# Ordering the gates in memory by group of four expert tiles

## What is computed

```python
    eidx = jnp.take_along_axis(cidx, pos, axis=-1)
    gates = jax.nn.softmax(top_s, axis=-1)
...
        u = jnp.take(u_tab, ib, axis=0)
        act = jax.nn.gelu(jnp.einsum('btd,bted->bte', hb, u), approximate=False)
        vv = jnp.take(v_tab, ib, axis=0)
        return jnp.einsum('bte,bted->btd', gb * act, vv)
```

## Time and profile before

| | |
|---|---|
| median of 3 runs | 2196.34 us (2192.71 to 2203.06) |
| profiled execution, its time / its span | 2198.44 us / 2196.6 us |
| TensorE busy in the span | 1880.5 us (86%) |
| VectorE busy | 1477.7 us (67%) |
| ScalarE busy | 729.6 us (33%) |
| moved by DMA | 411.22 MB in 160,491 packets |
| scatter stage's 12 writes | 994.5 to 1157.5 us (issue of first and last) |
| expert stage's gate loads | 1181.9 to 2111.4 us (issue of first and last) |

### The profile page before, as it was taken

The page is one execution under the profiler, slowest core; times in us unless marked ns, Lnnn a source line. Parts: engine busy times, 40 slices in busy tenths (PEclk is TensorE's granted clock), DMA queues, the critical chain, the costliest instruction groups (busy, mean ns, idle before and its releaser), DMA issues. The chain is left out here.

```text
span 2196.6 us, 33505 instructions
## 1 busy us (share of the span) xinstructions
PE 1880.5 (86%) x11429; PEld 1645.8 (75%) x11429; DVE 1477.7 (67%) x2682; ACT 729.6 (33%) x1060; POOL 709.8 (32%) x435
## 2 busy tenths in 40 slices
PE   2997678879986999968885998998998989989897
PEld 1765467768875999958874777787887878878797
DVE  5999544542313999999992667765766767768664
ACT  3235322233315444423432323332323323233233
POOL 1443111214442455521113222233443444435310
PEclk8999877779998999978997999999999998999999
DMA  7751000012222343324556888888888888788861
GB/s 298 261 180 48 1 2 0 0 38 94 97 77 77 132 136 131 123 76 169 191 205 245 310 294 297 295 284 307 279 265 296 275 305 279 263 311 283 296 212 57
DMA packets 160491, 411.22 MB, mean 187 GB/s; under 512 B 13496, under 2 KB 76088, under 8 KB 158784
## 3 DMA queue, kind: packets, MB, share of 16 engines
q1 hardware_dynamic: 115520, 264.13, 34.1%
q0 software_dynamic: 36864, 134.23, 18.6%
q10 hardware_dynamic: 8064, 12.32, 1.5%
HBM read 373.15 MB, written 37.49 MB: 187 GB/s over the span
## 5 line engine op out<-in xcount | busy, mean ns | idle before, releaser
L1645 PE MATMUL bank<-v_hi,coef_hi 128*128 128x512 f32 x768 | 305.0, 397 | 44.1 <-DVE coef_lo L1737 44.1
L1645 PE MATMUL bank<-v_hi,coef_lo 128*128 128x512 f32 x768 | 305.0, 397 | 0.0
L1645 PE MATMUL bank<-v_lo,coef_hi 128*128 128x512 f32 x768 | 304.9, 397 | 0.0
L1635 PE MATMUL bank<-h_hi,u_hi 128*128 128x384 f32 x608 | 220.1, 362 | 67.1 <-ACT gelu L1697 65.8
L1624 POOL DMA_INDIRECT own_rows<-in_u_rows_dram,own_row x128 | 154.8, 1209 | 349.6 <-DVE own_rows L1744 200.6
L1624 POOL DMA_INDIRECT own_rows<-in_peer_v_dram,own_row x128 | 189.8, 1483 | 230.4 <-DVE y_own L1801 217.4
L1635 PE MATMUL bank<-h_lo,u_hi 128*128 128x384 f32 x608 | 216.7, 356 | 0.0
L1635 PE MATMUL bank<-h_hi,u_lo 128*128 128x384 f32 x608 | 216.1, 355 | 0.0
L1737 DVE TENSOR_TENSOR v_lo<-v_tile,v_hi 128x1024 fp32r<-128x1024 f32 x128 | 156.2, 1220 | 76.5 <-ACT v_hi L1680 76.3
L1737 DVE TENSOR_TENSOR u_lo<-u_tile,u_hi 128x1024 fp32r<-128x1024 f32 x76 | 92.8, 1221 | 170.5 <-ACT u_hi L1674 170.5
L1645 PEld LDWEIGHTS bank<-v_hi,coef_hi 128*128 128x128 f32 x768 | 147.1, 192 | 78.0 <-issue 49.1
(11 more groups left out here) (326 smaller groups left out, 4106.2 us busy)
## 6 DMA issues: line engine op xcount, KB each, us to landing
v_tile<-in_peer_v_dram SPq DMA_DIRECT2D x128, 512.0 KB, 9.4
u_tile<-in_peer_u_dram SPq DMA_DIRECT2D x76, 512.0 KB
ada<-in_w_ada_dram SPq DMA_DIRECT2D x48, 512.0 KB, 4.9
gate_scratch<-gate_block SPq DMA_DIRECT2D x12, 2048.0 KB, 7.3
gate_tiles<-gate_scratch SPq DMA_DIRECT2D x32, 768.0 KB
piece<-in_peer_u_dram SPq DMA_DIRECT2D x36, 512.0 KB, 3.3
merge_w<-in_w_merge_dram SPq DMA_DIRECT2D x32, 512.0 KB, 3.3
wring<-in_w_proj_dram SPq DMA_DIRECT2D x28, 512.0 KB, 5.4
```

The lines of the kernel that those rows point to most:

```text
L1635: last = nc.tensor.matmul(bank[b][:, 0:TD], w[:, b, k, :], x[:, k, 0:TD], start=(k == 0 and n == 0), stop=(k == KT - 1 and n == 2))
L1645: last = nc.tensor.matmul(y_bank(t, half)[:], w[:, j, t * P:(t + 1) * P], x[:, j, c], start=(first and n == 0), stop=(final and n == 2))
```

## The change

`gate_scratch` keeps its size and contents, but not its order. Its axes were expert (partition), block of 32 tokens, tile, token. They are now expert, group of four tiles, block, tile in the group, token. A group's gates for one expert are so one contiguous piece of 12 x 4 x 32 x 4 bytes = 6 KB; before they were 12 pieces of 512 bytes. A block's gates for one expert were one piece of 16 KB and are now 32 pieces of 512 bytes, 6 KB apart.

```diff
-                        sp.dma_start(spill[:, bass.ds(i * SLOTS + slot, 1)], block_g[:, slot:slot + 1]).then_inc(stored[slot], 16)
+                        sp.dma_start(spill[:, :, bass.ds(i * SLOTS + slot, 1)].rearrange("p g o j t -> p (g o) j t"), block_g[:, slot].rearrange("p (g j) t -> p g j t", j=4)).then_inc(stored[slot], 16)
...
-                sp.dma_start(gt[:, 0], spill[:, :, 0:G, :]).then_inc(s_g[0], 16)
+                sp.dma_start(gt[:, 0], spill[:, 0]).then_inc(s_g[0], 16)
...
-                                sp.dma_start(gt[:, 1 - par], spill[:, :, bass.ds(i * G + G, G), :]).then_inc(s_g[1 - par], 16)
+                                sp.dma_start(gt[:, 1 - par:2 - par], spill[:, bass.ds(i + 1, 1)]).then_inc(s_g[1 - par], 16)
...
-SPILL = (P, TD // TB, P, TB)
+SPILL = (P, EXP_TILES // 4, TD // TB, 4, TB)
```

## The result

| | before | changed |
|---|---|---|
| median | 2194.26 us (6 runs) | 2157.77 us (6 runs) |
| ratio to before, 95% interval | | 0.9839 [0.9807, 0.9871] |
| profiled execution, its time / its span | 2198.44 / 2196.6 us | 2164.66 / 2162.8 us |

The kernel is 36 us, 1.6%, faster. The forecast was 70 us (2127 us, range 2085 to 2178).

A forecast was written before the change was run, and what follows sets the result against it. The prediction took late tiles behind each group's gate load to bound the expert stage. Early groups -24, late stalls -32, clock -14, head -2, write +2.4 sum to -70 us: about 2127 us, range 2085 to 2178.

The forecast's parts named there:

- What bounds the kernel: Expert stage: TensorE's stall is as long as the u tile behind the gate load is late, up to 4.1 us.
- The load, transfer, minus 0.6 us: Gate load in the expert stage: 6 KB runs priced like 4 KB runs take 2.0 us instead of 2.6.
- The load, start, minus 1.0 us: Gate load's beginning: flow starts 0.64 us sooner and the slow first slices, another 0.3 us, go.
- Both together, 1.6 us a load, 2.0 us a group: Expert stage: transfer and start save 1.6 us per load; with row fetches sharing engines, 2.0 us per group was taken.
- Early groups: First 12 groups between gate loads in the expert stage: 12 x 2.0 = 24 us saved, with room on TensorE.
- Clock, 14 us: Late groups: halving the stalls gives back 0.9 of 2.5 us a stall lost to the lower clock, 14 us.
- Head, minus 2 us: Start of the expert stage, two gate loads: bytes bind, so only transfer terms and some of the start count, 2 us.
- The write: Scatter stage: gate write lands at 9.7 us instead of 7.3; hidden in the loop, plus 2.4 us at the end.
- Signs of being wrong: Writes landing after more than 14 us, ScalarE's u waits staying near 197 us, or the stall moving to row fetches.
- Little comes through: Rival, expert stage: rows take the freed time, or the slow start belongs to contention; about 2168 us, chance 0.16.
- The other (2167): Rival, gate loads: 512 B runs already move at full rate, only start and issue shrink; 29 us gain, chance 0.04.
- More comes through: Rival, expert stage: 3.0 us a group where there is room, more clock, 8 us at the start; about 2080, chance 0.12.

The follow-up runs named there:

- quarter rows: Indexed row fetches, from the fifth on, cut to a quarter of a row: on the changed kernel 2070.36 us, on the kernel before 2069.22 us.

## Why the prediction was right, and where it was off

The path was right, the size was not: the gain is half of the forecast one. That the measured time lies in the range is owed to the range, which took in the small-gain cases.

- *What bounds the kernel*: right. The stall is as long as the u tile is late: it came 0.7 us sooner on the mean, and 16 stalls shrank by 10.8 us. Cutting the load moved the groups by as much as it cut and more.
- *The load, transfer, minus 0.6 us*: mis-sized. A 6 KB run was priced like a 4 KB run in a full stream, 24.5 bytes per ns. A load that starts alone gets 19.3, against 18.8 with 512 B runs. The transfer term is near nothing.
- *The load, start, minus 1.0 us*: half. The flow starts 0.45 us sooner, but the slow beginning did not go.
- *Both together, 1.6 us a load, 2.0 us a group*: this is the step that was off. The load's own gain is 0.5 us alone. The u tile behind it comes 1.0 us sooner at the last load, 1.1 us in the late groups with quarter rows, and 0.7 us in the late groups of this kernel. In the other three kernels with full new loads in the old place and full row fetches that tile came after 11.0 to 11.1 us on the mean, and after 12.3 and 12.4 in the two with the old loads, so 0.7 to 1.5 us is what the change is worth there. The groups got 1.0 us (early, 11.9/12) and 1.4 us (late, 22.2/16 stalls), clock included; of stalls alone the late ones got 0.7 us, where 2.0 were forecast.
- *Early groups*: beside the size, the forecast didn't ask what is late next. It is the second v tile, at 11.8 us.
- *Clock, 14 us*: nearly right by number, and by luck. TensorE's busy time in the late stretch fell by 11.6 us, at a mean granted clock of 0.95 instead of 0.94. But the forecast had it from stalls that halve, and they shrank by a sixth; for the early groups, where busy time fell by 5.5 us (0.98 instead of 0.96), it had no such term.
- *Head, minus 2 us*: -0.6. SyncE's 8.00 us at the v tile did go (1.09 us now), worth nothing, as bytes bind there (DMA share 0.97 before and 0.95 now).
- *The write*: priced right (9.7 us forecast, 9.2 measured), and hidden in the loop as said. The tail was mis-sized, 5.0 instead of 2.4 us. The u_early tile lands 3.5 us later and not 2.4; SyncE is held for 5.3 us in issuing it behind the 4096 runs, which may be the reason, but no run shows that. The remaining 1.5 us fit the lower clock of the matmuls behind the stall.
- *Signs of being wrong*: the forecast named ScalarE's waits for u staying near 197 us. They went to 186.5, which is nearer to that than to a gain of 2.0 us a group, and the groups went to 18.3 and 38.0 us, not to 17.3 and 36.4.
- *Rivals*: two came nearer than the forecast. "Little comes through" (2168) did by its number; its cause, that the row fetches take the freed time, is not borne out, since the load without them gains less than forecast too. The other (2167), to which I gave 4%, has the better mechanism: runs of 512 B already move as fast as longer ones, so that only start and issue shrink, 1.0 us a group. The Trainium skill (DMA: Bandwidth & Descriptors, Specifications) puts the least transfer for line rate at 512 B. For a load alone the trace agrees in so far as longer runs gained hardly any engine time, 19.3 against 18.8 bytes per ns. "More comes through" and the slow write did not occur; the write runs flowed at some 290 GB/s.

## What to carry to other kernels

In this kernel a transfer that waits for late work holds everything that is issued behind it on its queue. Ask first whether it can be issued later, and only then whether it can be made faster: moving one condition was worth 6%, reordering the array 1.6%, and both together no more than the first. Price a short DMA by what a DMA alone shows in its first microseconds, not by the rate of a full stream, and price a longer write by who stands behind its last instance.

## What the runs showed of the hardware

- A 768 KB load at rest took about the same engine time in 128 runs of 6 KB as in 1536 of 512 B (19.3 and 18.8 bytes per ns); the longer runs began 0.45 us sooner and crept for some 0.8 us.
- The write of 4096 runs of 512 B flowed at 284 to 295 GB/s, that of 16 KB runs at 1.85 MB in 5 us, 370 GB/s. From 991 to 998 us in the changed kernel (slices of 0.175 us):

```profile
GB/s 0 0 0 0 184 295 290 295 284 290 287 293 287 295 290 293 290 290 290 287 295 287 293 290 287 295 290 290 290 287 293 290 293 290 287 295 290 287 287 293
```

- SyncE is held in the issue behind a DMA of many runs: 5.0 to 5.3 us for u_early behind each new write, 0.34 us behind the old one.
